# A streaming encoder step with routed experts on one core: projection, attention and merge moved from the front of the program into the expert loop, three tiles at a time

## The reference, cut to what matters

```
h = rmsnorm(x); q_sb,k_sb,v_sb,q_sw,k_sw,v_sw,q_mem,gates = split(h @ w_in)
branch A  stick-breaking attention, 8 heads x 64, strictly causal:
          z = q.k/8 ; log_keep = -softplus(z) ; weight = exp(log_sigmoid(z) + later log_keeps)
branch B  sliding window over the last two 64-chunks, 8 q heads, 2 kv heads, softmax with a sink
branch M  4 heads x 128 into 256 memory tokens, softmax
x += w_out( sum_b sigmoid(gate_b) * (o_b @ w_o_b) )
xn = rmsnorm(x); q = xn @ w_q ; s = q . keys        (8 heads, 2 x 128 keys)
top 16 of each half, top 16 of their 256 sums -> 128 expert ids and weights per token
x += sum_k weight_k * gelu(u_k . xn) * v_k          (16384 experts, u and v of 1024 values)
```

## Time and profile before

| | |
|---|---|
| time, median of 3 runs | 4207.86 us (4206.48 to 4216.56) |
| profiled execution: its own time | 4207.44 us |
| profiled execution: span in the trace | 4205.6 us |
| mean granted TensorE clock | 0.870 of full speed |
| PE / DVE / ACT / POOL busy | 77% / 58% / 30% / 26% of the span |
| DMA | 1399.44 MB, mean 333 GB/s |
| first gather issued | at 1044.4 us |
| table loads of ACT | 62, of 1283 ns each |

### The profile page before, as it was taken

One profiled execution on the slowest core, in us unless ns is written; L12 is line 12 of the kernel. 1 busy time (PEld: TensorE's weight loads), 2 busy tenths in 40 slices (PEclk: granted clock), 3 DMA queues, 4 the chain that ended last, 5 costly groups with the idle time before them and its releaser, 6 DMA issues.

```text
span 4205.6 us, 46334 instructions
## 1 busy us (share of the span) xinstructions
PE 3254.9 (77%) x16665; PEld 1443.1 (34%) x16665; DVE 2448.8 (58%) x5586; ACT 1249.4 (30%) x3959; POOL 1098.0 (26%) x1167
## 2 busy tenths in 40 slices
PE   8999999898779998778888887985555555555555
PEld 4545665587424454322222242431111111111111
DVE  2131456512957756857757765785775775776444
ACT  2111467601422223322222224332222222222222
POOL 0000000000333323333333333333333333333332
PEclk9999899999889999989999998987777777777777
DMA  4301320044999999999999999999999999999998
GB/s 139 113 20 66 122 76 16 21 163 158 419 420 420 415 414 417 393 421 421 420 417 421 419 414 421 421 396 417 421 418 417 417 411 413 419 413 417 421 421 342
DMA packets 242087, 1399.44 MB, mean 333 GB/s; under 512 B 26544, under 2 KB 54448, under 8 KB 89008
## 3 DMA queue, kind: packets, MB, share of 16 engines
q0 software_dynamic: 165888, 1208.03, 69.6%
q1 hardware_dynamic: 75968, 188.44, 12.1%
HBM read 1366.49 MB, written 30.80 MB: 332 GB/s over the span
## 4 chain that ended last, share of the span: by engine, by line
DMA 38%; PE 22%; DVE 14%; issue 3%; ACT 2%; POOL 1%; another core or an unknown queue 0%; DVEq 0%; ACTq 0%; POOLq 0%
DMA ring<-in_experts_dram,idx 38%; PE ps L1416 10%; DVE ring L1674 6%; PE ps L1340 4%; PE ps L1388 4%; PE ps L1365 2%; PE ps L1350 2%; ACT diag L1510 1%; DVE hot L1564 1%; DVE hot L1560 1%; DVE idx L1568 1%; POOL ring L1311 1%; ACT wgt L1504 1%; DVE flat L1556 1%; DVE flat L1553 1%
## 5 line engine op out<-in xcount | busy, mean ns | idle before, releaser
L1416 PE MATMUL ps<-ring,diag 64*64 64x512 f32 x9216 | 1445.0, 757 | 870.1 <-ACT diag L1510 856.9
L1674 DVE CUSTOM_DVE_ANT_0 ring<-ring,ps 128x1024 f32<-128x1024 f32 x1152 | 1390.3, 1220 | 962.8 <-DMA ring<-in_experts_dram,idx 902.0
L1311 POOL DMA_INDIRECT ring<-in_experts_dram,idx x1152 | 1092.0, 948 | 2665.5 <-PE ps L1416 1900.8
L1416 PEld LDWEIGHTS ps<-ring,diag 64*64 64x64 f32 x9216 | 356.1, 159 | 1868.8 <-ACT diag L1510 1298.3
L1497 ACT ACTIVATE act_<-hid 128x2 f32<-128x2 f32 x576 | 117.2, 204 | 2075.8 <-DVE hid L1674 2008.9
L1340 PE MATMUL ps<-shared 128*128 128x256 f32 (+2 forms) x1152 | 409.3, 502 | 5.5 <-PEq L535 4.5
L1510 ACT ACTIVATE diag<-const,wgt 128x64 f32<-128x64 f32 x1152 | 337.9, 340 | 18.8
L1340 PEld LDWEIGHTS ps<-shared 128*128 128x128 f32 x1152 | 215.1, 194 | 207.3 <-issue 151.0
L315 PE MATMUL ps<-shared,hT 128*128 128x512 f32 (+1 forms) x720 | 284.8, 551 | 1.8 <-DVE mhT L429 1.3
L1504 ACT ACTIVATE wgt<-act_,gw 128x1 f32<-128x1 f32 x1152 | 276.7, 287 | 20.6 <-ACT act_ L1497 0.4
L1388 PE MATMUL ps<-shared 128*128 128x256 f32 (+2 forms) x768 | 273.6, 505 | 1.2 <-ACT shared L1459 1.2
(11 more groups left out here) (178 smaller groups left out, 2512.4 us busy)
## 6 DMA issues: line engine op xcount, KB each, us to landing
shared<-in_w_gate_o_dram SPq DMA_DIRECT2D x72, 768.0 KB
shared<-in_w_q_dram SPq DMA_DIRECT2D x24, 1024.0 KB
ring<-in_experts_dram,idx POOLq DMA_INDIRECT x1152
shared<-in_w_out_dram SPq DMA_DIRECT2D x12, 1024.0 KB
shared<-in_w_in_dram SPq DMA_DIRECT2D x5, 2048.0 KB, 8.1
o_x<-o_scratch SPq DMA_DIRECT2D x9, 768.0 KB
hT_scratch<-hT SPq DMA_DIRECT2D x9, 512.0 KB, 6.5
shared<-hT_scratch SPq DMA_DIRECT2D x9, 512.0 KB
```

Of the source, the lines that this page charges most:

```text
L1311: i = nc.gpsimd.indirect_dma_start(out=ring[:, j % RING, :], out_offset=None, in_=A["experts"], in_offset=bass.IndirectOffsetOnAxis(ap=idx ...
L1416: last = nc.tensor.matmul(acc[ROWS[r ^ h], h, :], diag[ROWS[r], j % 4, :], ring[ROWS[r], j % RING, DM + h * HB:DM + (h + 1) * HB], start=( ...
L1674: last = nc.vector.tensor_tensor_reduce(out=u, in0=u, in1=xp, scale=1.0, scalar=0.0, op0=ALU.mult, op1=ALU.add, accum_out=hid[:, j % SLOTS ...
```

## The change

The three blocks become one (`layer`). The nine tiles are taken in the order 0, 1, ST, 2, 3, 4, 5, 6, 7, in three groups of three. For each group the steps of `Proj` (a list in place of the loops of `project`), of `Course` and of `Front` follow one another in one chain, and `advance` takes the next steps from that chain. The first group's project, attend and 109 of its 140 front steps run ahead of the first gather. The steps of a later group (245 and 279) are dealt out between the ticks of the group before it, 1.55 and 1.52 for a tick.

What else changes with it:

- The weights of the projection are loaded once for each group; the scratch copies of h and of the attention's outputs in DRAM are gone.
- `RING` is 7 in place of 10, and the ring's memory holds caches while the first group is in work. `xp`, the normalized row that the dot products read, lies in SBUF in place of PSUM. The pool of the gathers' descriptors is 8192 bytes a partition.
- In `attend` a key block takes four steps in place of two (`PACE = 4`), there are two halves of PSUM in place of four and one `za` in place of two.
- Square roots on ACT become Ln and Exp with three refining operations on DVE (`refine`).
- In the ticks of `EXP_FORM`, in which steps of a later group's project or attend fall (160 of 576: ticks 26 to 93 and 192 to 283), the GELU is formed of Exp, Ln and Exp on ACT and four small operations on DVE, in place of one activation.
- The line `preload_act_table_set` is gone and nothing stands in its place.

```
-RING = 10
+RING = 7
-GROUPS = ((0, 1), (2, 3, 4), (5, 6, 7, 8))
+ORDER = (0, 1, ST, 2, 3, 4, 5, 6, 7)
+TILES_OF = tuple(ORDER[N * g:N * g + N] for g in range(NGROUPS))
...
-            nc.scalar.preload_act_table_set("natural_log_exp_and_others")
...
+LENGTH = [J.length[g] + C.length[g] + FRONTS[g].steps for g in range(NGROUPS)]
+def paces():
+    total = [sum(LENGTH[:g + 1]) for g in range(NGROUPS)]
+    done = J.length[0] + C.length[0] + FRONTS[0].first_head
...
-            chain = (0 for f in FRONTS for _ in front(f))
+            chain = (0 for g in range(NGROUPS) for stage_of in (project, attend, front) for _ in stage_of(g))
...
+                    if EXP_FORM[T]:
+                        n_exp += 1
+                        nc.scalar.activation(act_[:, c], act_[:, c], ACT.Exp, scale=-GELU_B).then_inc(gelus, 1)
+                        act.wait_ge(gelus, T + 1)
+                        nc.scalar.activation(act_[:, c], act_[:, c], ACT.Ln, bias=1.0).then_inc(logged, 1)
+                        act.wait_ge(logged, n_exp)
+                        nc.scalar.activation(act_[:, c], act_[:, c], ACT.Exp, scale=-1.0).then_inc(sigmas, 1)
...
-                nc.scalar.activation(nrm[:, 1, 0:H], nrm[:, 0, 0:H], ACT.Sqrt).then_inc(rooted, 1)
+                        nc.scalar.activation(nrm_h[:, 2, 0:H], nrm_h[:, 1, 0:H], ACT.Ln).then_inc(mean_ln, 1)
+                        act.wait_ge(mean_ln, n)
+                        nc.scalar.activation(nrm_h[:, 2, 0:H], nrm_h[:, 2, 0:H], ACT.Exp, scale=-0.5).then_inc(inverted, 1)
...
+                    if EXP_FORM[T]:
+                        link(last)
+                        c = recent(tick)
+                        link(nc.vector.scalar_tensor_tensor(out=cube[:, 0, :], in0=hid[:, c], scalar=GELU_A, in1=hid[:, c], op0=ALU.mult, op1=ALU.mult))
+                        nc.vector.tensor_tensor(gx[:, c], hid[:, c], gw[:, m % 2, tick * BATCH:(tick + 1) * BATCH], ALU.mult)
+                        link(nc.vector.scalar_tensor_tensor(out=cube[:, 1, :], in0=cube[:, 0, :], scalar=1.0, in1=hid[:, c], op0=ALU.add, op1=ALU.mult))
+                        last = nc.vector.tensor_scalar(act_[:, c], cube[:, 1, :], -GELU_FAR, None, ALU.max)
```

More of the change, by code:

```diff
@@ new lines, with exp_form @@
+PACES = paces()
+def exp_form():
+    at, spans = 0, []
+    for g in range(NGROUPS):
+        spans.append((at, at + J.length[g] + C.length[g]))
+        at += LENGTH[g]
+    out, done = [], PACES[0]
+    for T in range(NT * NB):
+        to = done + PACES[1 + T]
+        out.append(any(done <= b and to > a for a, b in spans[1:]))
+        done = to
+    return out
+EXP_FORM = exp_form()
+TOP_AT = {m: (m - 1) * NB + (30 if m == 1 else 18 if m == 2 else 6) for m in range(1, NT) if m not in FIRST_OF}
@@ L577, in attend @@
         vw_in = sem("vw_in")
-        km_in = [sem(f"km_in{i}") for i in range(3)]
+        km_in = [sem(f"km_in{i}") for i in range(KM)]
         mul_done = sem("mul_done")
@@ L1322, in _, with turn @@
         def _(pe):
-            def front(f):
-                g, n, N = f.g, f.n, f.cols
+            def turn(u):
+                n = J.n_turn[u] - 1
+                if n >= 1:
+                    pe.wait_ge(kept, n)
+                if J.units[u][1] == "ksb":
+                    pe.wait_ge(copied, J.n_copy[u])
+                else:
+                    pe.wait_ge(gained, J.n_norm[u])
+                m = 1 if J.units[u][1] == "kvsw" else 4
+                for j in range(m):
+                    last = nc.tensor.transpose(ps[:, 5, j * P:(j + 1) * P], stage[:, J.slot[u], j * P:(j + 1) * P], ident)
+                last.then_inc(turned, 1)
@@ new lines, in project @@
+            def project(g):
+                for tau in range(J.length[g]):
+                    key = (g, tau)
+                    if key in J.turn_x:
+                        i = J.turn_x[key]
+                        n = J.x0[g] + i
+                        if n == 0:
+                            pe.wait_ge(const_in, 16)
+                        pe.wait_ge(x_nat, n + 1)
+                        if i:
+                            pe.wait_ge(h_done, n)
+                        elif g:
+                            pe.wait_ge(s_kept, PH * g)
+                        for c in range(KC):
+                            last = nc.tensor.transpose(ps[:, 6 + c // 4, (c % 4) * P:(c % 4 + 1) * P], xt[i][:, c * P:(c + 1) * P], ident)
+                        last.then_inc(x_T, 1)
+                    if key in J.turn:
+                        turn(J.turn[key])
+                    if key in J.part:
+                        produce(*J.part[key])
+                    yield
@@ L1325, in front @@
+            def front(g):
+                f = FRONTS[g]
+                n = f.n
                 for tau in range(f.steps):
```

2261 lines of the change are left out of this document (1124 added, 1137 removed).

## The result

The changed kernel takes 5004.26 us (median of four runs, 5001.74 to 5008.88) against 4207.86 us for the kernel before (median of three, 4206.48 to 4216.56). A fourth run of before, at 9722 us, is left out of the comparison; the ratio of the others is 1.1887, 95% interval 1.1864 to 1.191. The forecast was 5020 us, 19% slower. The profiled execution has a span of 4999.9 us and took 5001.74 us.

A forecast was written before the change was run, and what follows sets the result against it. It took TensorE as the bound up to 1044 us and DMA after that. Front 641, lead 156, EXP_FORM ticks 2001, merge 1128, gathers only 1063, ring 25, tail and own time 9 sum to 5023; forecast 5020 us, range 4500 to 5330.

The forecast's parts named there:

- projection ticks: 63 ticks carrying a later group's projection steps: 10.2 us each, 643 us in all.
- attention ticks: 97 ticks carrying a later group's attention steps: 14.0 us each, 1358 us in all.
- The front: First group's stages ahead of the first gather: projection 188, attention 160, merge 293, sum 641 us against 1044.
- Table loads: ScalarE's function table loads: 600 against 63, 1.283 us each, two uncovered between Exp, Ln and Exp of a tick.
- Rival 3: Table loads cost nothing or are not run: ticks of 10.2 and 8.0 us, total 4480 us; chance 0.10.
- The chain A + accumulation + step: EXP_FORM tick as a serial sum: ScalarE's part A 4.4 us, accumulation 1.95 us, then the dealt-in step's pieces.
- the clock: TensorE under 40% busy in attention ticks gets a lower granted clock; 0.5 us a tick added.
- Merge and plain ticks, lead: 182 merge ticks at 6.2 us, gather-only ticks at 5.11 us, and 26 ticks after the first gather, 156 us.
- The ring: Seven gather slots in place of ten leave less time for a gather in flight: 25 us, bounds 0 and 150.
- Rival 1: Engines overlap better than chain sums: ScalarE floor 7.4 us a tick, half way 10 us, total 4620 us; chance 0.14.
- rival 2: Faster than before: ticks with attention or projection steps take a merge tick's 6.2 us, total 4014 us; chance 0.03.
- Rival 4: Gathers suffer from seven slots and dots with both inputs in SBUF: 0.5 us in 390 ticks, 5220 us; chance 0.10.

The follow-up runs named there:

- one_table: Changed kernel with the table set holding both exp and ln loaded once ahead of the first group and of each EXP_FORM run; 4514.4 us.
- steps_first: Changed kernel with TensorE's dealt-in steps issued ahead of the tick's accumulation, not behind it, in the 160 EXP_FORM ticks; 4564.4 us.
- both: Changed kernel with one table set for exp and ln, and TensorE's steps ahead of the accumulation in EXP_FORM ticks; 4201.6 us.
- lag_attend: Changed kernel with one table set, ScalarE's steps ahead of its exponentials, TensorE's steps ahead of accumulation, which comes a tick late in attention ticks only; 4129.9 us.
- lag_only: Changed kernel with one table set and TensorE's accumulation a tick late, behind the next tick's steps, in EXP_FORM ticks; 4262.4 us.
- gelu_one: Changed kernel with the Gelu function in all 576 ticks and the exp-and-ln set reloaded behind the diagonals of 160 ticks; 4526.2 us.

## Why the prediction was right

The total was within 0.4% and the experiments bear the mechanism out: a tick of EXP_FORM is one chain, with the table loads and the accumulation on it. That the total is so close is partly luck. The projection ticks were 55 us below the forecast and the attention ticks 47 above, and inside both other errors cancel.

- **The front** (641; 641.3). It is right by cancelling terms: projection 188 against 175, merge 293 against 280 (361 to 641.3 us), attention 160 against 186. The attention of group 0 was 26 us too short in my sum. TensorE's clock there was 0.71; I had priced its products at rows of a stage with 0.90, and hold that for the likely cause without a run that shows it.
- **Table loads.** 600, 1.283 us each, as forecast (the trace of before has 63; the table ahead of the prediction says 62). Rival 3's sums (10.2 and 8.0 us a tick, 4480 us) are what a kernel without them should take: one_table took 10.74, 7.48 and 4514. The price of the loads, 540 us in my sums, was 490.
- **The chain A + accumulation + step.** A is 4.4 us on the timeline as summed. The mis-sized term is the clock: I added 0.5 us a tick for it, and the one tick shown above lost 2.7 us to it in accumulation and products. In the first attention stage L1177 is busy 128.64 us in 37 ticks, 3.5 us each, 1.5 more than at the full clock, and the scores and products can slow down too. That the attention tick still came out at 14.5 and not above 15 means that other parts of the chain overlapped by about as much as this added. So 14.0 was right by two errors that nearly cancel. Which parts overlapped is not shown. steps_first, priced from the same chain, saved 440 us and not 290: I had taken only the accumulation off the path, and the products left it too.
- **Projection ticks** (10.2; 9.33). Which kind of tick was shorter than its sum is not shown; I take it that the double ticks overlap more than I allowed. one_table's 7.48 is close to the 7.2 us that TensorE alone needs.
- **Merge and plain ticks, lead.** 6.21, 5.09 and 5.94 against 6.2, 5.11 and 6.0: work read from rows of the same kind of tick carries over. Counted from the first gather, as the forecast did, the lead takes 165.5 us and not 156, because the first dot product starts 11 us behind that gather.
- **The ring.** 25 us forecast, 25 measured in the kernel before. The 25 was picked between bounds of 0 and 150 and not worked out, so its closeness is luck; in the changed kernel the term was not measured by itself.
- **Rival 1** (engines overlap) and **rival 2** (6.2 us a tick) did not come about in this order. That it is the order and the loads, and not the work, is shown by both and lag_attend, which do the same work at 7.5 and 7.0 us a tick. The floor that I set rival 1 was near: ScalarE is busy for 1159 us in the four stages, 7.2 us a tick against my 7.4.
- **Rival 4.** The contention is there and has no price. The Trainium skill ("SBUF — State Buffer", Who interferes with whom) has a VectorE instruction with two SBUF inputs contend with a GpSimd instruction that reads SBUF; 946 to 1098 ns agrees. Two such instructions fill 2.2 us of a tick of 5.1, so nothing waits for them.

Left open: how the 127 us between the sum of the two single savings and both divide over the clock and VectorE's steps; why lag_only is slower than both in the attention; and what the clock alone is worth, since no run changes it without changing the waits.

## What to carry to other kernels

When work with its own waits is dealt into the idle time of a loop, write down for each engine what is queued behind each wait; idle engines do not help if the slot's own chain is one of the links. Price the chain at the clock that the slowed loop will be granted, not at that of the busy loop it comes from. And decide the order of steps stage by stage: ScalarE's steps first gained 37 us in one kind of tick and lost 95 in the other.

## What the runs showed of the hardware

- Exp and Ln one after the other cost a table load of 1.283 us at each turn unless the set that holds both is loaded ahead: 600 loads became 49 by naming that set once ahead of each run.
- Where a table load stands in program order does not say whether it is covered: in gelu_one 89 of 158 loads issued ahead of the wait for the dots were not covered at all, because the dots were already done, while a load behind the diagonals was followed by 4.79 us of waiting for TensorE. The kernel has 316 more loads than one_table and takes 12 us longer.
- The granted clock was higher where TensorE waited less: the same attention work had 0.69, 0.78 and 0.85 in the changed kernel, steps_first and both (first attention stage), where TensorE waited 299, 122 and 58 us for diagonals. The accumulation of one tick took 3.69 us at the lower and 1.95 us at the upper level.
- A dot product with both inputs in SBUF takes as long as one with an input in PSUM (1225 against 1220 ns, medians), while the gather instruction beside it grows from 946 to 1098 ns in the mean: about a quarter of them take 1.1 to 2.0 us, and half stay at 0.94 or less.
